# First mixer of a two-block transformer kernel: modulation steps one condition at a time and spread, a buffer of its own for their first chunk, two parts of the first weight group run early

## The reference, cut to what matters

```python
silu_c, silu_cc = jax.nn.silu(c)[:, None, :], jax.nn.silu(c_ctx)
for i in range(DEPTH):                                  # 4 layers
    sh_a, sc_a, g_a, sh_m, sc_m, g_m = split(silu_c @ mod_w[i] + mod_b[i], 6)
    # the same with silu_cc for the context, where the context is still updated
    h = modulate(x, norm_mix_g[i], sh_a, sc_a)          # rms_norm * g * (1 + sc) + sh
    y = mixer(h)                                        # layers 0 and 3: Fourier
    x = x + g_a * y
    x = x + g_m * sq_relu_mlp(modulate(x, norm_mlp_g[i], sh_m, sc_m), mlp_w1[i], mlp_w2[i])

def fourier_mixer(h, w, bias):                          # 4 groups of 256 channels
    f = fft2(h in groups, axes=(tokens, channels of the group), norm="ortho").real
    return f @ w + bias
```

## Time and profile before

| what | us |
|---|---|
| three runs | 2960.28, 2960.62, 2963.84 |
| their median | 2960.62 |
| the profiled execution, device time | 2960.59 |
| its span, first to last instruction | 2959.3 |
| TensorE busy in the span | 2892.5 (98%) |
| VectorE busy | 1934.1 (65%) |
| ScalarE busy | 1471.0 (50%) |
| GpSimd busy | 1094.5 (37%) |

### The profile page before, as it was taken

How to read it: one execution, slowest core, us unless ns; L and a number is a source line. 1 busy time by engine, 2 the same in 40 slices (tenths; PEclk the granted TensorE clock), 3 DMA queues, 4 the chain that set the end, 5 groups by cost and what they waited for, 6 DMA issues and landing times.

```text
span 2959.3 us, 48992 instructions
## 1 busy us (share of the span) xinstructions
PE 2892.5 (98%) x19914; PEld 2564.9 (87%) x19914; DVE 1934.1 (65%) x3391; ACT 1471.0 (50%) x2520; POOL 1094.5 (37%) x484
## 2 busy tenths in 40 slices
PE   7999999999999999999999999999999999999999
PEld 6788887877788886599999987889999988899999
DVE  3877775666576645666665576676466776775676
ACT  3453333444443323655555457665465466654653
POOL 0422222000322232045645542444555533444554
PEclk9999999999999999999999999999999999999999
DMA  8555652211357642058745542444555533435554
GB/s 283 185 176 195 199 199 86 73 58 42 100 193 266 245 173 64 30 182 263 248 128 178 185 141 90 117 126 143 172 173 176 167 118 109 120 124 185 180 189 136
DMA packets 404846, 459.95 MB, mean 155 GB/s; under 512 B 8720, under 2 KB 381584, under 8 KB 404624
## 3 DMA queue, kind: packets, MB, share of 16 engines
q1 hardware_dynamic: 401536, 453.41, 47.5%
q10 hardware_dynamic: 3088, 3.42, 0.4%
HBM read 455.75 MB, written 1.05 MB: 154 GB/s over the span
## 4 chain that ended last, share of the span: by engine, by line
PE 91%; DVE 5%; ACT 2%; issue 1%; DMA 1%; POOL 0%; ACTq 0%; DVEq 0%; POOLq 0%
PE bank L446 26%; PE bank L448 25%; PE bank L447 25%; PE banks L446 1%; PE banks L448 1%; PE banks L447 1%; PE bank L1545 1%; PE banks L1556 1%; PE banks L2844 1%; DMA X<-in_ctxT 1%; PE banks L1893 1%; DVE wl L406 1%; PE banks L1882 1%; PE bank L1872 1%; PE bank L1875 1%
## 5 line engine op out<-in xcount | busy, mean ns | idle before, releaser
L421 POOL TENSOR_TENSOR wl<-raw,wh 128x768 fp32r<-128x768 f32 (+3 forms) x324 | 926.6, 2861 | 1605.4 <-ACT wh L387 1605.4
L387 ACT ACTIVATE wh<-raw 128x2048 fp32r<-128x2048 f32 (+1 forms) x336 | 636.1, 1893 | 471.4 <-PE bank L448 387.5
L406 DVE TENSOR_TENSOR wl<-raw,wh 128x1280 fp32r<-128x1280 f32 (+3 forms) x332 | 504.4, 1519 | 353.1 <-ACT wh L387 352.9
L446 PE MATMUL bank<-nh,wh 128*128 128x272 f32 (+1 forms) x1552 | 453.9, 292 | 4.9 <-DVE y L2582 3.3
L448 PE MATMUL bank<-nh,wl 128*128 128x272 f32 (+1 forms) x1552 | 446.0, 287 | 0.0
L446 PE MATMUL bank<-xh,wh 128*128 128x512 f32 (+2 forms) x1282 | 441.1, 344 | 4.2 <-DVE xl L802 3.7
L447 PE MATMUL bank<-nl,wh 128*128 128x272 f32 (+1 forms) x1552 | 444.4, 286 | 0.0
L448 PE MATMUL bank<-xh,wl 128*128 128x512 f32 (+2 forms) x1282 | 434.0, 339 | 0.0
L447 PE MATMUL bank<-xl,wh 128*128 128x512 f32 (+2 forms) x1282 | 433.8, 338 | 0.0
L446 PE MATMUL bank<-hh,wh 128*128 128x512 f32 (+1 forms) x1024 | 344.1, 336 | 0.0
L447 PE MATMUL bank<-hl,wh 128*128 128x512 f32 (+1 forms) x1024 | 344.1, 336 | 0.0
(11 more groups left out here) (522 smaller groups left out, 5830.7 us busy)
## 6 DMA issues: line engine op xcount, KB each, us to landing
raw<-in_mlp_w SPq DMA_DIRECT2D x128, 1024.0 KB, 5.5
raw<-in_w_in SPq DMA_DIRECT2D x60, 1024.0 KB, 5.3
raw<-in_mod_wT SPq DMA_DIRECT2D x48, 1024.0 KB, 5.5
extra<-in_mod_wT SPq DMA_DIRECT2D x36, 1024.0 KB, 5.2
raw<-in_w_mlp_up SPq DMA_DIRECT2D x32, 1024.0 KB, 5.4
raw<-in_w_mlp_down SPq DMA_DIRECT2D x32, 1024.0 KB, 4.9
raw<-in_w_in SPq DMA_DIRECT2D x34, 512.0 KB, 5.0
raw<-in_w_ssd_down SPq DMA_DIRECT2D x16, 1024.0 KB, 4.9
```

What stands on the lines that cost most here:

```text
L387: nc.scalar.activation(self.wtile(self.wh, c1), self.rawtile(c1), AF.Copy).then_inc(*up("act_wh", ("wh", c1)))
L406: nc.vector.tensor_tensor(l, r, h.bitcast(F32), ALU.subtract).then_inc(*up("dve_wl", ("wl_dve", c1), *([("wl_pool", c1)] if n == self.P[c1 ...
L421: nc.gpsimd.tensor_tensor(l, r, h.bitcast(F32), ALU.subtract).then_inc(*up("pool_wl", ("wl_pool", c1), *([] if n else [("wl_dve", c1)])))
L446: nc.tensor.matmul(o, ah, bh, start=first, stop=False)
```

## The change

It has six parts, all in the first mixer but for the last.

1. The first dmod chunk (12) gets a buffer of its own, `extra2`, in the place that `ah` and `al` leave free by lying closer together. It had used the third raw buffer, after mod chunk 10. On SyncE its transfer keeps its place, without a wait for that buffer.
2. The conditions are spread in steps 2 (condition 0) and 4 (condition 1), not 4 and 5.
3. A dmod piece is now issued by `dve_start_halves`, one condition at a time. The 32 pieces have new places: two in step 3, ahead of that step's end, one at the start and one at the end of step 4, one each in steps 6 and 7, and in the weights' stage four each before the first two residuals and three each before the other six. Before, there were two each in steps 5, 6 and 7 and four in step 8, and in the stage 4, 2, 4, 2, 4, 2, 2 and 2. Chunk 12 is done for condition 0 first, the others for condition 1 first.
4. `act_lambda` and `dve_lambda` go from step 4 into the weights' stage.
5. ScalarE splits the weight chunks 0, 1 and 2 in steps 5, 7 and 8, not in 5, 8 and 8.
6. Parts 0 and 2 of the first weight group run in the last step, ahead of fb; the other six parts of that group follow where the group was (`pe_fw_part`). The groups of the first mixer now use the banks in the order 2, 3, 0, 1. The new function is not tied to L = 0: in layer 3 the two parts go ahead of the last fb too, in step 4.

The core of the diff:

```diff
+                if c == dmods[0]:
+                    t = EXTRA2
...
+        if L == 0:
+            self.extra2 = self.mem("extra2", 2048, F32, o + 8192)
...
-                if n in (4, 5):
-                    self.pe_condition("mix0", n - 4, 0)
-                    self.pe_condition("mix0", n - 4, 1)
+                if n in (2, 4):
+                    self.pe_condition("mix0", n // 2 - 1, 0)
+                    self.pe_condition("mix0", n // 2 - 1, 1)
...
+                if n == 4 * S:
+                    self.pe_fw_part(L, S, (0, 2))
                 b = self.pe_bank((0, 1) if L == 0 else RING, "fb", L, n - 1)
...
+                if j == 0 and m == 0:
+                    self.pe_fw_part(L, S, (4, 6, 1, 3, 5, 7))
+                else:
+                    self.pe_group(c, m, slot, Y, slice(0, 256 * S), ("fw", L, 2 * j + m), m == 1, ks=(0, 2, 4, 6, 1, 3, 5, 7), of=self.fw_banks(L))
+
+    def fw_banks(self, L):
+        return RING if L else (2, 3, 0, 1)
+
+    def pe_fw_part(self, L, S, ks):
+        at, up, PE = self.T.at, self.T.up, self.PE
+        fh, fl = self.four[L][5:7]
+        T = slice(0, 256 * S)
+        h, l = self.pe_take(self.ix["fw", L, 0])
+        if ks[0] == 0:
+            self.pe_bank(self.fw_banks(L), "fw", L, 0)
+        o = self.place["fw", L, 0][:, T]
+        for k in ks:
+            PE.wait_ge(*at("yh", L, S - 1, k))
+            PE.wait_ge(*at("yl", L, S - 1, k))
+            ins = self.mm3(o, h[:, k, 0:128], l[:, k, 0:128], fh[:, k, T], fl[:, k, T], k == 0, k == 7)
...
-            if L == 0 and n in (5, 8):
-                self.act_split(self.ix["fw", L, 0 if n == 5 else 2], 1)
-            if L == 0 and n == 4:
-                self.act_lambda()
+            if L == 0 and n in (5, 7, 8):
+                self.act_split(self.ix["fw", L, (0, 1, 2)[n - 6] if n > 5 else 0], 1)
...
+            if L == 0 and n == 4:
+                self.dve_start_halves(1)
...
-                if n >= 5:
-                    self.dve_start_dmods(2 if n == 8 else 1)
+                self.dve_start_halves((0, 0, 0, 2, 1, 0, 1, 1, 0)[n])
...
-                    self.dve_start_dmods((2, 1, 2, 1, 2, 1, 1, 1)[k])
+                    self.dve_start_halves(4 if k < 2 else 3)
+                    if k == 3:
+                        self.dve_lambda()
...
+    def dve_start_halves(self, n):
+        nc, at, up, DVE = self.nc, self.T.at, self.T.up, self.DVE
+        steps = [(12, m, s) for s in (0, 1) for m in range(2)] + [(i, m, s) for i in range(13, 20) for m in range(2) for s in (1, 0)]
         for _ in range(n):
+            i, m, s = steps[self.start_dmods]
+            c, again = self.ix["dmod", 0, i], s == (0 if i == 12 else 1)
...
+            DVE.wait_ge(*at("raw", c))
+            DVE.wait_ge(*at("cb", "mix0", s, 0))
+            DVE.wait_ge(*at("cb", "mix0", s, 1))
+            if again:
+                if self.junked is not None:
+                    DVE.wait_ge(*at(*self.junked))
+                self.junked = "half", i, m, s
```

More of the change, by code:

```diff
@@ L31 @@
 EARLY = 8
-EXTRA = 8
+EXTRA, EXTRA2 = 8, 9
 RING = (0, 1, 2, 3)
@@ L346, in rawtile @@
         _, _, kt, n, _ = self.P[c]
-        return (self.raw + self.early + [self.extra])[self.home[c]][:, 0:kt * n]
+        return (self.raw + self.early + [self.extra, self.extra2])[self.home[c]][:, 0:kt * n]
     def sp_load(self, upto):
@@ L1014, in fourier_memory @@
         tl = self.tiles(f"tl{n}", 2, 644, F32R, o + 49152 + 5152)
-        ah = [self.tiles(f"ah{n}{i}", 2, 256, F32R, o + 8192 * i) for i in range(2)]
-        al = [self.tiles(f"al{n}{i}", 2, 256, F32R, o + 8192 * i + 4096) for i in range(2)]
+        ah = [self.tiles(f"ah{n}{i}", 2, 256, F32R, o + 4096 * i) for i in range(2)]
+        al = [self.tiles(f"al{n}{i}", 2, 256, F32R, o + 4096 * i + 2048) for i in range(2)]
+        if L == 0:
+            self.extra2 = self.mem("extra2", 2048, F32, o + 8192)
         fh = self.tiles(f"yh{n}", 8, 512, F32R, o + 16384)
@@ L1125, in pe_fourier @@
             for m in range(2):
-                self.pe_group(c, m, slot, Y, slice(0, 256 * S), ("fw", L, 2 * j + m), m == 1, ks=(0, 2, 4, 6, 1, 3, 5, 7))
+                if j == 0 and m == 0:
[16 more added lines that the diff above has]
+            ins = self.mm3(o, h[:, k, 0:128], l[:, k, 0:128], fh[:, k, T], fl[:, k, T], k == 0, k == 7)
+        if ks[-1] == 7:
+            ins.then_inc(*up("pe_acc", ("acc", "fw", L, 0)))
     def pe_nyquist_shift(self, L, s):
@@ L1236, in act_fourier @@
             self.act_split(self.ix["fw", L, j])
+            if L == 0 and j == 1:
+                self.act_lambda()
             if L == 0 and j < 2:
@@ L1309, in dve_fourier @@
                 if n == 4:
-                    self.dve_lambda()
                     self.dve_fourier_bias(L)
-                if n >= 5:
-                    self.dve_start_dmods(2 if n == 8 else 1)
+                self.dve_start_halves((0, 0, 0, 2, 1, 0, 1, 1, 0)[n])
         for j in range(4):
@@ L1318, in dve_fourier @@
                 if L == 0:
-                    self.dve_start_dmods((2, 1, 2, 1, 2, 1, 1, 1)[k])
+                    self.dve_start_halves(4 if k < 2 else 3)
+                    if k == 3:
+                        self.dve_lambda()
                 DVE.wait_ge(*at("xb", L, k))
                 self.dve_resid(("fw", L, k), L, 2, k, T, f"mlp{L}")
-    def dve_start_dmods(self, n):
+    def dve_start_halves(self, n):
+        nc, at, up, DVE = self.nc, self.T.at, self.T.up, self.DVE
+        steps = [(12, m, s) for s in (0, 1) for m in range(2)] + [(i, m, s) for i in range(13, 20) for m in range(2) for s in (1, 0)]
         for _ in range(n):
-            i, m = 12 + self.start_dmods // 2, self.start_dmods % 2
-            self.dve_dmod(self.ix["dmod", 0, i], m)
+            i, m, s = steps[self.start_dmods]
             self.start_dmods += 1
+            c, again = self.ix["dmod", 0, i], s == (0 if i == 12 else 1)
+            w = self.rawtile(c).rearrange("p (m k) -> p m k", m=2)[:, m, :]
+            DVE.wait_ge(*at("raw", c))
[5 more added lines that the diff above has]
+                self.junked = "half", i, m, s
+            done = m == 1 and not again
+            nc.vector.tensor_tensor_reduce(out=self.junk[:] if again else w, in0=w, in1=self.cb[s][:], scale=1.0, scalar=self.col("mod_b", 2 * i + m), op0=ALU.mult, op1=ALU.add,
+                                           accum_out=self.modv[:, 0, 2 * i + m, s:s + 1]
+                                           ).then_inc(*up("dve_dmod", ("modv", 0, i) if done else ("half", i, m, s), *([("used", c)] if done else []),
+                                                          *([("out", "cb", "mix0", s, 0), ("out", "cb", "mix0", s, 1)] if (i, m) == (19, 1) else [])))
     def pool_fourier(self, L, S):
```

## The result

| | median, us | runs | ratio to the kernel before, 95% interval |
|---|---|---|---|
| before | 2960.73 | 2957.31 to 2963.84 | |
| with the change | 2965.04 | 2960.49 to 2968.75 | 1.0014 (1.0009 to 1.0020) |

A forecast was written before the change was run, and what follows sets the result against it. TensorE, busy 98%, was taken as the bound, with gains only where it waits, 76 to 92 us. 4.2 won - 1.6 clock - 1.2 VectorE - 0.7 layer 3 = 0.7 us less: 2959.9, range 2955.8 to 2963.2.

The forecast's parts named there:

- The stand and its fall: Step 4: TensorE waits 3.5 us for VectorE to free bank 7; one half-rate clock stretch then costs 1.6 us.
- The early parts: Step 8: six early weight products, 1.4 us, fill TensorE's 1.36 us wait for `yl`; the 2.31 us wait goes too.
- The even start: Start of the weights' stage with an even clock: 88.3 in place of 92.5, 4.2 us won.
- VectorE in the weights' stage: VectorE's list starts 3.8 us behind the even start; the last residual comes 1.2 us after TensorE, a loss.
- 40.7 of work: VectorE's work in the weights' stage in us: 40.4 before, plus `dve_lambda` (0.3).
- Layer 3: Six early products ahead of fb push fb and VectorE's last low parts back: cost 0.7 us.
- the third case: Rival, weights' stage: chunk waits make VectorE the bound, 4.5 us behind TensorE; 2963.2 us, chance 0.14.
- The clock's swinging on: Rival: step 6's 0.9 us wait and the stand bring two clock falls; 2961.5 us, chance 0.12.
- No idle over 1 us: Sign: TensorE has no idle time over 1 us from step 5 to the first weight product.

The follow-up runs named there:

- e4: The kernel before with only the early weight parts, in layer 0 alone, and ScalarE's split a step earlier: 2958.28 us, ratio 0.9988.
- e11: The changed kernel with e1's and e2's edits, early parts in layer 0 alone, ScalarE's bias additions of steps 5 to 8 behind step 8: 2954.02 us, ratio 0.9982.
- e2: The changed kernel with the low parts of the first two MLP chunks wholly on GpSimd: 2959.64 us, ratio 0.9993.
- e6: The changed kernel with the low parts of the first two MLP chunks wholly on VectorE: 2965.57 us, ratio 1.0012.
- e7: The kernel before with the low parts of the first two MLP chunks wholly on GpSimd: 2960.42 us, ratio 0.9996.
- e1: The changed kernel with the two pieces of step 3 moved behind step 4's adding up: 2962.09 us, ratio 1.0000.
- e10: The changed kernel with seven unused products where TensorE stands for bank 7: 2965.42 us, ratio 1.0017.

## Why the prediction was wrong, by its own steps

- **The stand and its fall** held: 3.39 us for 3.5, and behind it one fall of the clock. Step 5 begins at 75.92 for 75.7.
- **The early parts** held: the waits of 1.36 and 2.31 us are gone, and e4 shows the gain by itself.
- **The even start** failed in size. TensorE's last weight product is 1.03 us earlier, counted from step 2, where 4.2 - 1.6 = 2.6 were forecast. From step 5 on I took one wait, 0.9 us ahead of step 6's fa; it did not come. There were two others: 0.84 in step 5 (the edge row's low parts, which hold fb's bank) and 0.98 ahead of step 7 (`nyq`, behind ScalarE's split and bias, as e11 shows), a step whose pieces I took to fit. That 0.84 is near 0.9 is luck. From start to start the two put the products behind them 1.00 and 1.12 us back, 1.2 more than forecast; 0.2 is step 5's later start, and the rest lies in the stage itself.
- **VectorE in the weights' stage** failed in its mechanism. The list did begin 3.8 us behind the even start, as forecast. But "40.7 of work" took each `wl` at the length it had when VectorE came first. Later on its list it came second, and the two cost 1.94 us more. I had looked for the loss in transfers (0.43 us in fact, 0.6 forecast); the rest of the list took 0.7 less than the sum has it. The last residual came 2.33 us behind the end of TensorE's last product, before 0.10: 2.23 lost, not 1.2. e2, e6 and e7 show this.
- **What follows the last residual** was missing from the sum. With VectorE late, TensorE idles 3.3 us ahead of the norm, and in this trace the clock falls on the norm's products: 9.64 us from the last residual to the first MLP product where before it took 144.63 - 136.44 = 8.19, so 1.45 lost. Over the fourteen traces: with 3.1 to 3.3 us of idle time it is 9.64 (the change and e4), 10.74 (e1) and 9.53 (e6), but 8.17 in e10; with 1.1 or less it is 8.17 to 8.19 in all nine. So the fall came in four of five, and why it stayed away in e10 is open.
- **Layer 3**: 0.72 for 0.7. The new wait shows as small gaps: the first group's parts behind the edge row begin 0.42 to 0.68 us apart, where before most stood at 0.36.

Together 1.57 + 1.03 + 1.45 = 4.05 us of mixer that the forecast (1.4 won) missed, against 2.65 lost: all of it, for the two traces. 2.65 + 0.72 = 3.4; the other 0.9 of the median's 4.3 is within its interval, and falls of the clock elsewhere are as large.

Of the rivals the third case's number (VectorE as the bound, 2963.2) was nearest, but for another reason than the chunks. The clock's swinging on, the fourth case, did not come in steps 5 to 8: behind 0.84 and 0.98 us it stayed at 1.00. "No idle over 1 us" from step 5 to the weights held, just.

## What to carry to other kernels

When an edit lets one engine start a stage earlier, work out which engine ends the stage then, and count the time of its instructions anew: a duration read beside a neighbour that came second is not the duration when the neighbour comes first. If two engines share a tile and exclude each other, giving the tile to the one with slack can be worth more than the order of the work (3.7 us here, nothing while the other engine is the bound). And price the idle time at the end of a stage with what the clock may do behind it: 1.35 to 2.56 us here, in four traces of five.

## What the runs showed of the hardware

VectorE's subtraction of two SBUF tiles and GpSimd's don't overlap: 1.49 and 3.15 us, or 2.74 and 1.84, by who begins first. The pieces, which read one input from PSUM, don't take part: with the change, GpSimd's tile at 107.84 took 4.64 us beside three of them, and the one at 83.15, beside a single one, 4.59. And in the traces of these kernels, alike from the first MLP on but for the fourth layer's mixer, the granted clock falls at two to six places between 700 and 1870 us, not the same ones in each; the two new ones of the changed kernel cost 1.45 us each. A difference of 2 us between two traces can be that. What brings such a fall there, no run here shows.
